# Two chains of heads in lockstep: the second one 35 phases behind the first in place of 18, its heads filled up to 51 phases

## What is computed

```python
def _gla_scan(q, k, v, log_f, s0):          # forget gate, per head, chunk by chunk
    bc = jnp.cumsum(gc, axis=-2)
    s_new = jnp.exp(b_last)[..., None] * s + einsum('bhsk,bhsv->bhkv', kc * exp(b_last - bc), vc)
    att = einsum('bhtk,bhsk,bhtsk->bhts', qc, kc, w)     # w = exp(bc_t - bc_s) below the diagonal
    o = einsum('bhtk,bhkv->bhtv', qc * exp(bc), s) + einsum('bhts,bhsv->bhtv', att, vc)
def _delta_scan(q, k, v, g, beta, s0):      # delta net, per head, chunk by chunk:
    ...                                     # a triangular system (I + A) is inverted, then a state loop
```

## Time and profile before

| | us |
|---|---|
| device time, median of 3 (4926.59 to 4939.75) | 4931.92 |
| device time of the profiled execution | 4934.87 |
| its span | 4933.4 |
| the stage of the two chains within it (2541.3 to 3501.4) | 960.1 |

### The profile page before, as it was taken

One profiled execution on the slowest core, in us unless ns is written; L12 is line 12 of the kernel. 1 busy time (PEld: TensorE's weight loads), 2 busy tenths in 40 slices (PEclk: granted clock), 3 DMA queues, 4 the chain that ended last, 5 costly groups with the idle time before them and its releaser, 6 DMA issues.

```text
span 4933.4 us, 69710 instructions
## 1 busy us (share of the span) xinstructions
PE 4316.6 (87%) x28096; PEld 3667.4 (74%) x28096; DVE 2810.2 (57%) x5619; ACT 1548.4 (31%) x2683; POOL 0.2 (0%) x4
## 2 busy tenths in 40 slices
PE   7598899699999989999877778777778897999997
PEld 7333223689999978889767777777645797999997
DVE  4756444566556542234557777777632476655654
ACT  3211111444444432234122222222100243444442
POOL 0000000000000000000000000000000000000000
PEclk9799999899999999999789899998989999999999
DMA  5344555346565654457451112121422463655653
GB/s 174 96 147 147 169 163 155 121 153 190 187 187 180 192 149 120 115 147 208 120 150 51 55 52 58 50 58 40 127 70 75 156 200 116 192 187 185 186 188 112
DMA packets 383056, 669.52 MB, mean 136 GB/s; under 512 B 43897, under 2 KB 77402, under 8 KB 382220
## 3 DMA queue, kind: packets, MB, share of 16 engines
q1 hardware_dynamic: 327168, 595.74, 40.2%
q10 hardware_dynamic: 55564, 69.31, 4.3%
HBM read 634.87 MB, written 29.46 MB: 135 GB/s over the span
## 4 chain that ended last, share of the span: by engine, by line
PE 63%; DVE 13%; issue 2%; ACT 2%; DMA 1%; ACTq 0%; DVEq 0%
PE acc L547 13%; PE acc L549 12%; PE acc L548 12%; PE acc L589 8%; PE bank L548 2%; PE bank L547 2%; PE bank L549 2%; PE bank L1654 2%; PE bank L1663 2%; PE bank L1661 1%; ACT weights_hi L511 1%; PE bank L2130 1%; DVE arena L1493 1%; PE acc L1462 1%; PE bank L734 1%
## 5 line engine op out<-in xcount | busy, mean ns | idle before, releaser
L526 DVE TENSOR_TENSOR weights_lo<-weights_ring,weights_hi 128x512 fp32r<-128x512 f32 x1600 | 1094.1, 691 | 1022.5 <-ACT weights_hi L511 1020.9
L511 ACT ACTIVATE weights_hi<-weights_ring 128x512 fp32r<-128x512 f32 x1600 | 994.3, 630 | 1078.8 <-PE acc L549 882.3
L548 PE MATMUL acc<-arena_halves,weights_hi 128*128 128x256 f32 (+2 forms) x3136 | 916.3, 292 | 0.0
L547 PE MATMUL acc<-arena_halves,weights_lo 128*128 128x256 f32 (+1 forms) x2944 | 860.4, 292 | 21.7 <-DVE weights_lo L526 12.2
L549 PE MATMUL acc<-arena_halves,weights_hi 128*128 128x256 f32 (+1 forms) x2944 | 858.8, 292 | 0.0
L547 PE MATMUL acc<-moving_halves,weights_lo 128*128 128x256 f32 (+1 forms) x2816 | 792.1, 281 | 73.0 <-DVE weights_lo L526 72.3
L549 PE MATMUL acc<-moving_halves,weights_hi 128*128 128x256 f32 (+1 forms) x2816 | 786.6, 279 | 0.0
L548 PE MATMUL acc<-moving_halves,weights_hi 128*128 128x256 f32 x2624 | 731.4, 279 | 0.0
L548 PEld LDWEIGHTS acc<-arena_halves,weights_hi 128*128 128x128 f32 x3136 | 590.5, 188 | 12.1
L547 PEld LDWEIGHTS acc<-moving_halves,weights_lo 128*128 128x128 f32 x2816 | 535.7, 190 | 81.6 <-DVE weights_lo L526 53.6
L589 PE MATMUL acc<-moving,weights_ring 128*128 128x256 f32 x2304 | 581.2, 398 | 10.4 <-ACT arena L692 9.3
(11 more groups left out here) (422 smaller groups left out, 4830.9 us busy)
## 6 DMA issues: line engine op xcount, KB each, us to landing
weights_ring<-in_w_in SPq DMA_DIRECT2D x624, 256.0 KB, 2.7
weights_ring<-in_w_ff SPq DMA_DIRECT2D x512, 256.0 KB, 3.0
weights_ring<-in_w_ada SPq DMA_DIRECT2D x384, 256.0 KB, 2.9
weights_ring<-in_w_up SPq DMA_DIRECT2D x256, 256.0 KB, 2.9
weights_ring<-in_w_down SPq DMA_DIRECT2D x256, 256.0 KB, 3.2
weights_ring<-in_w_out SPq DMA_DIRECT2D x128, 256.0 KB, 3.2
weights_ring<-in_w_branch SPq DMA_DIRECT2D x96, 256.0 KB, 3.3
s_state<-arena ACTq DMA_DIRECT2D x36, 256.0 KB, 2.8
```

What stands on the lines that cost most here:

```text
L511: a.activation(whi, k.slot(g.ring0 + kc), ACT.Copy).then_inc(*s.made("scalar_done", "high", n))
L526: v.tensor_tensor(wlo, k.slot(g.ring0 + kc), whi.bitcast(F32), ALU.subtract).then_inc(*s.made("vector_done", "low", n))
L547: pe.matmul(g.out[m], wlo[:, cols], xhi, start=first, stop=False, skip_group_check=g.shared)
L548: pe.matmul(g.out[m], whi[:, cols], xlo, start=False, stop=False, skip_group_check=g.shared)
```

## The change

```diff
     for head in range(8):
         before = [end(k, name, head - 1)] if head else []
-        yield from lockstep(before + [strand(k, r, head) for r in range(2)] + [start(k, head)])
+        phases = 0
+        for _ in lockstep(before + [strand(k, r, head) for r in range(2)] + [start(k, head)]):
+            phases += 1
+            yield
+        for _ in range(51 - phases):
+            yield
     yield from end(k, name, 7)
 
 def heads2(k, hg_start, forget, dn_start, delta, end, whole):
-    chains = [chain(k, "hg", hg_start, forget, end), chain(k, "dn", dn_start, delta, end, 18)]
-    beside(lockstep(chains), 414, [...])
+    chains = [chain(k, "hg", hg_start, forget, end), chain(k, "dn", dn_start, delta, end, 35)]
+    beside(lockstep(chains), 444, [...])
```

More of the change, by code:

```diff
@@ L1936, in chain @@
         before = [end(k, name, head - 1)] if head else []
-        yield from lockstep(before + [strand(k, r, head) for r in range(2)] + [start(k, head)])
+        phases = 0
[4 more added lines that the diff above has]
+            yield
     yield from end(k, name, 7)
 def heads2(k, hg_start, forget, dn_start, delta, end, whole):
-    chains = [chain(k, "hg", hg_start, forget, end), chain(k, "dn", dn_start, delta, end, 18)]
-    beside(lockstep(chains), 414, [(whole(k, g), 36) for g in k.some("read", 11, 12) + k.some("gates", *range(6))])
+    chains = [chain(k, "hg", hg_start, forget, end), chain(k, "dn", dn_start, delta, end, 35)]
+    beside(lockstep(chains), 444, [(whole(k, g), 36) for g in k.some("read", 11, 12) + k.some("gates", *range(6))])
 def heads2_tensor(k):
```

## The result

| | before | after |
|---|---|---|
| device time, median of 19 | 4936.87 | 4949.95 |
| lowest and highest | 4926.59 to 4952.46 | 4942.36 to 4965.15 |
| profiled execution, its span | 4934.87, 4933.4 | 4947.47, 4946.0 |
| the stage of the two chains | 960.1 | 967.8 |

The ratio after to before is 1.0026, with a 95% interval of 1.0017 to 1.0036: 13 us slower. The forecast was 4916, 16 us faster, with a range up to 4940. The sign was wrong, and the time lies outside the range.

What follows compares the result with a forecast made beforehand. The stage was taken as bound by turns of TensorE and VectorE: 50.7 + 795.9 + 99.0 + 1 = 946.6 us, 13.5 below 960.1. With a second estimate of 23, 16 less was taken: 4916, range 4899 to 4940.

Steps and rivals of the forecast that it cites:

- bound by turns: Stage of the two chains, 960.1 us: TensorE busy 743, VectorE 732, neither filling it; each leads in different stretches.
- The background: Background matmuls over 444 phases in place of 414: 0.04 us less a phase, 0.6 in fourteen level phases.
- the fourteen level phases of a round: Delta net level passes beside forget-gate levels, outside the starts: bound by TensorE, 28.1 us a round.
- The level phases beside the forget gate: Delta net level passes beside the forget gate: 2.05 us a phase in rounds, 2.01 in the last delta net head.
- Starts beside level passes: First ten phases of a forget-gate head beside delta net level passes: 39.5 us, between 37.5 and 44.
- The second rival: Level passes beside a start wait in ScalarE's queue and for TensorE: 42 us a start, no change within 5; chance 0.25.
- The wait in phase 2: TensorE's wait for VectorE in phase 2 of a forget-gate head: near 10 us, shortened from 16.7.
- the third rival: TensorE at half clock from phase 2's end through the next level pass: 35 us in all, 19 slower, 4951; chance 0.1.
- First eight phases of the delta net: Start of each delta net head, where VectorE leads: 22.5 us, and 16.9 in head 0.
- The state loop: Fourteen delta net phases beside forget-gate levels: 15.4 us a round, 16.0 less 0.6 for the background.
- The stretch behind the last forget-gate end: From the last forget-gate end to the stage's end: 44 us, against 6 before the change.
- The second estimate: Larger of VectorE's and TensorE's time over blocks of eight phases, 923 before, 891 after; with some 9 off, 23 us less.

Runs made afterwards that it cites:

- pieces414: The changed kernel with the background spread over 414 phases again, distance 35 and filling kept: ratio to before 0.9979, stage 952.3 us.
- after_warm: The changed kernel with 22 idle matmuls added behind phase 2 of forget-gate heads 1 to 7: ratio to before 1.0015, stage 973.7 us.
- the gathered background: 12 times the background in phases 1 to 3 of each forget-gate head, added to after (ratio to before 0.9965, stage 948.8) and to before (0.9932, 929.1).
- after_copy: The changed kernel with the sigmoid of the first six gate groups replaced by a plain copy: ratio to before 1.0015, stage 967.8 us.

## Why the prediction was wrong, step by step

- *That the stage is bound by turns* is right, and every run rests on it; level passes with TensorE full are there too (27.60 of 27.60). The blind side was that I applied it to the two chains only and took the third, the background, as even.
- *The background* is the step that failed: "this is bound by TensorE, so the thinner background counts here", 0.04 us less a phase. The mean got thinner, and the full phases 40 to 51 got thicker, from 29.2 to 55.8 us of background in seven heads. The price is 15.5 us in the stage. In the forecast's own terms it is the fourteen level phases of a round, 28.1 us each time and 196.7 in seven rounds. With the background over 414 phases they take 194.2, so the term was right for that place of the empty steps; over 444 they take 210.7, and the background in them goes from 39.28 us to 60.49. The chance that the change of 414 to 444 does harm stood among no rivals, although the text of the code names the four last steps of a group without a matmul, and 414/8 beside 52 could be read from it. Before the change the same windows would have shown it: background in phases 40 to 51 of before is 31.84 us for 84 phases, 0.38 a phase, where an even spread of 1024 records of 0.23 us over 414 phases is 0.57.
- *The level phases beside the forget gate*, 2.05 or 2.01 us each, came from rows of delta net head 3, which lie beside the forget gate's phases 17 to 40, not beside its state loop. Twelve such phases were measured at 27.6 us in head 7, 2.30 each; with the empty steps in them, in pieces414, 23.7, 1.98 each. The rate was right only for the old place of the empty steps.
- *Starts beside level passes*, the term named as the unknown, was 39.5 with ends of 37.5 and 44. It is 42.7 in after and 42.3 in pieces414 (296.2/7): inside the bounds, but 3.2 us above the value taken, seven times, 22 us in all: the second term that was mis-sized, and the larger one. VectorE's work was as forecast, its waits were 6.5 us in place of 3.0. (The mean of 35.5 and 38.4 is 37.0, not 36.5.) The second rival's 42 us a start was met; its total, no change, was not met by the kernel that has these starts without the other fault, pieces414, at 0.9979.
- *The wait in phase 2* was to be 10 us: it is 9.4 in head 1 and 11.3 to 17.6 in the other six, 14.8 in the mean. So the argument against the third rival, that the pass before shortens the idle time from 16.7 us to some 10, failed. *The clock*, the third rival, is seen where it was foretold (0.50 on the "both" matmuls), and the sign that the prediction set for it, starts of 42 us or more with a clock of 0.50 behind phase 2, was there. Its forecast total of 4951 was hit to a microsecond. That is luck: the price would have been there in pieces414 too, which has the same distance and much the same waits and is faster than before. A total that fits, and even a sign that fits, is no evidence for a mechanism's price. What part of the 22 us in the starts is the clock's no run here shows, since after_warm left the clock behind the wait as low as it was.
- *The first 35 phases* 47.4 for 50.7. *First eight phases of the delta net* 20.4 to 22.5 in heads 1 to 7 for 22.5. *The state loop* 13.4 to 16.4 for 15.4. *The stretch behind the last forget-gate end* 41.5 for 44. These terms held, mostly on the safe side. The sum of 946.6 was missed by 21.2 us: 22.4 more in the starts, 14.0 more in the level phases, and 15.2 less in the rest.
- *The second estimate*, by blocks of eight phases (23 us less), had the background spread evenly in it as well, so it could not warn. A second look that shares an assumption with the first doesn't widen the range as it should.
- *That the distance gains* is right in sign: 0.9979 and 0.9983 are 8 to 10 us, where 13.5 was the sum and 16 the forecast. *That the filling keeps no constant distance* is right, and it is worth nothing that can be told.

What is open: how the 3.5 us more of VectorE's waiting in a start divide between the clock, ScalarE's queue and the order of the matmuls, why the gathered background gained less in after than in before, and the few microseconds between differences of stages and of whole times.

## What to carry to other kernels

When work is dealt out evenly over a schedule, compare the period of its own uneven pieces with the period of what it lies beside: 51.75 against 52 gave 960.1 us and 952.3, 55.5 gave 967.8, and the same density ten phases later gave 985.7 and 979.2. Rather than tune such a number, write down where filler goes: into phases where its engine waits for another, and out of those where it is full; that was worth five times as much as aligning the chains (38 us against 7). And when a change sets three numbers, cost each alone, the one that looks like an adjustment too.

## What the runs showed of the hardware

Two things were not expected. Idle work in TensorE's wait raised the mean granted clock of a stretch and not the clock of the work behind the wait: in head 1 of after_warm 10.9 us of idle matmuls and the "left" matmuls ran, a wait of 4.4 us followed, and the next matmuls had a granted clock of 0.50 again; the means of the seven starts rose by 0.08 to 0.18 all the same. A mean over a stretch doesn't tell at which clock the matmuls ran that others wait for. And loads of ScalarE's tables, 1.283 us each, do not show in the stage's time: with 23 of them taken out (after_copy) it is 967.8 as with them, though ScalarE's copies stand in the chain between TensorE's matmuls. The Trainium skill, in ScalarE: Activation LUTs, What ACT_TABLE_LOAD costs, gives about 1283 ns for the load and some 1380 ns more for a drain. The first agrees with the rows; the second isn't seen in this trace, where the function starts right behind its load:

```profile
2628.03 1.28 ACT L1575 ACT_TABLE_LOAD   x1
2629.32 1.15 ACT L1575 ACTIVATE arena<-arena 128x512 f32<-128x512 f32 x2
```
